# Second block's mixing on one NeuronCore: scans placed among the projections, attention by groups of heads with one row per query, and the output projection in two halves of its inputs

## The reference, cut to what matters

```python
proj = h @ w_in                  # a_q a_k a_v | cq ckv kr | z xbc dt
y_a = diff_attention(a_q, a_k, a_v, lam, subln_g)   # 4 heads, q and k of 32+32, v of 64
y_b = mla(cq, ckv, kr, ...)                         # 4 heads, q and k of 64+32, v of 64
y_c = mamba2(z, xbc, dt, ...)                       # 8 heads of 64
y = concatenate([y_a, y_b, y_c]) @ w_out            # 256 + 256 + 512 inputs
x = x + g * rmsnorm(y)
```

## Time and profile before

| | |
|---|---|
| Median of 3 runs | 3539.12 us (3535.72 to 3542.89) |
| Profiled execution: its own time | 3541.45 us |
| Profiled execution: span | 3539.7 us |
| PE busy | 3192.5 us (90%) |
| DVE busy | 1755.1 us (50%) |
| POOL busy | 832.0 us (24%) |
| ACT busy | 705.4 us (20%) |
| Mean granted PE clock | 0.913 |

### The profile page before, as it was taken

One profiled execution on the slowest core, in us unless ns is written; L12 is line 12 of the kernel. 1 busy time (PEld: TensorE's weight loads), 2 busy tenths in 40 slices (PEclk: granted clock), 3 DMA queues, 4 the chain that ended last, 5 costly groups with the idle time before them and its releaser, 6 DMA issues.

```text
span 3539.7 us, 33580 instructions
## 1 busy us (share of the span) xinstructions
PE 3192.5 (90%) x12312; PEld 2192.8 (62%) x12312; DVE 1755.1 (50%) x3758; ACT 705.4 (20%) x1539; POOL 832.0 (24%) x704
## 2 busy tenths in 40 slices
PE   6877989999987788999979998899997998899996
PEld 3334548888733454888864452488884444378886
DVE  1375337775327543777542265495833347152343
ACT  2233320000113332000012241220202133121110
POOL 0120113444312011344430000144340000124442
PEclk8987799999998788999999978899998978899998
DMA  4111313443211001344221100144420210112221
GB/s 194 57 39 72 143 60 113 173 179 110 90 48 48 24 1 60 130 156 183 106 76 67 71 1 0 72 172 161 179 103 28 76 48 1 48 48 95 77 91 48
DMA packets 38546, 304.89 MB, mean 86 GB/s; under 512 B 4192, under 2 KB 4320, under 8 KB 23920
## 3 DMA queue, kind: packets, MB, share of 16 engines
q1 hardware_dynamic: 38352, 302.68, 23.3%
q0 software_dynamic: 32, 0.07, 0.0%
HBM read 300.63 MB, written 2.10 MB: 86 GB/s over the span
## 4 chain that ended last, share of the span: by engine, by line
PE 78%; DVE 11%; issue 4%; ACT 3%; DMA 2%; POOL 1%; DVEq 0%; SPq 0%; POOLq 0%; ACTq 0%
PE bank L950 43%; PE bank L928 16%; PE bank L1039 4%; PE bank L1294 1%; DVE SPT L2265 1%; PE bank L1147 1%; PE bank L1089 1%; PE bank L1278 1%; PE bank L1076 1%; PE bank L1026 1%; DMA ring<-in_slabs 1%; DVE sel L1931 1%; PE bank L1285 1%; PE bank L1013 1%; DVE m L1930 1%
## 5 line engine op out<-in xcount | busy, mean ns | idle before, releaser
L855 POOL TENSOR_TENSOR SPT<-ring 128x512 f32<-128x512 f32 (+2 forms) x140 | 170.3, 1216 | 1863.3 <-DMA ring<-in_slabs 1244.6
L928 PE MATMUL bank<-hT,ring 128*128 128x512 f32 (+1 forms) x960 | 422.2, 599 | 14.6 <-ACT hT L1604 6.5
L950 PE MATMUL bank<-U,ring 128*128 128x256 f32 x1728 | 406.5, 380 | 0.0
L950 PEld LDWEIGHTS bank<-U,ring 128*128 128x128 f32 x1728 | 326.3, 190 | 43.3
L928 PEld LDWEIGHTS bank<-hT,ring 128*128 128x128 f32 (+1 forms) x960 | 181.3, 190 | 252.1 <-issue 246.1
L1750 DVE SCALAR_TENSOR_TENSOR nw<-sel,c,nw 128x256 f32<-128x256 f32 x504 | 321.8, 638 | 23.2 <-DMA sel<-in_mod_pieces 5.5
L950 PE MATMUL bank<-hT,ring 128*128 128x256 f32 x1216 | 299.8, 397 | 22.4 <-ACT hT L1604 8.6
L950 PE MATMUL bank<-U,SPT 128*128 128x256 f32 x1296 | 311.2, 379 | 0.1
L950 PE MATMUL bank<-hT,SPT 128*128 128x256 f32 x1216 | 287.3, 379 | 0.0
L950 PEld LDWEIGHTS bank<-hT,ring 128*128 128x128 f32 x1216 | 230.3, 195 | 70.9 <-issue 17.2
L950 PEld LDWEIGHTS bank<-U,SPT 128*128 128x128 f32 x1296 | 246.2, 190 | 33.9 <-POOL SPT L860 0.5
(11 more groups left out here) (293 smaller groups left out, 4164.6 us busy)
## 6 DMA issues: line engine op xcount, KB each, us to landing
ring<-in_slabs SPq DMA_DIRECT2D x88, 2048.0 KB, 8.0
sel<-in_mod_pieces SPq DMA_DIRECT2D x144, 512.0 KB, 3.8
ring<-in_slabs SPq DMA_DIRECT2D x8, 1536.0 KB, 7.1
ring<-in_slabs SPq DMA_DIRECT2D x8, 1280.0 KB, 6.0
ring<-in_slabs SPq DMA_DIRECT2D x4, 1664.0 KB, 7.0
ring<-in_slabs SPq DMA_DIRECT2D x2, 1808.0 KB, 7.3
cst<-in_consts SPq DMA_DIRECT2D x1, 2120.0 KB, 24.3
ring<-in_slabs SPq DMA_DIRECT2D x2, 1056.0 KB, 5.3
```

What stands on the lines that cost most here:

```text
L855: pool.tensor_tensor(e1, a21, a22, ALU.add).then_inc(*pool_order.up())
L928: mm = pe.matmul(dst, lhs(k), rhs(k), start=(k == 0), stop=(k == n - 1))
L950: mm = pe.matmul(into[j][:, c:c + HALF], lhs[:, k, :], rhs[:, k, :], start=(begin and k == 0), stop=(end and k == kp - 1))
```

## The change

1. **Order.** `proj` 6 to 9, 4 and 5 come first, then `projv`, then `proj` 0 to 3, 10 to 13 and the mla steps ("dense") are woven with all the scan steps ("scans"). Then `proj` 14 to 17 are woven with `sz`, `sn` and the first six attention slots (the mla groups), and the remaining slots (the 12 diff groups) with the first half of the output projection.
2. **Attention by groups.** 6 mla groups and 12 diff groups of 1 to 4 heads instead of 32 units. No multiplication of the weights by 1/sum: for mla the output is scaled; for diff one combination `cb` per head forms `e1 + c e2`. The value product has one row per query (weights stationary), outputs are normed per query (square on ACT, reduction on DVE, Ln and Exp on ACT, `on` on DVE) and turned back by `ot`.
3. **Output projection** in two halves of its inputs: `("wo", 0, n)` takes the four scan tiles, ACT copies it; `("wo", 1, n)` takes the attention outputs, DVE adds it. Squares are summed by POOL, with one matmul at the end, for `post` 0 as for `post` 1.
4. **Banks.** PROJ (0, 1) for projections; `da` has bank 2 alone, `xd` and `G` bank 3; `y` alternates over 4 and 5; `pv` has bank 6 alone, `ot` and `sn` bank 7. Mixing matrices are packed, three heads deep. Slabs are repacked (`bv` of 4160 columns, `mix` of 1280) and come in another order.

```diff
+GROUPS2 = [("m", 0, 4, 0), ("m", 0, 4, 1), ("m", 0, 2, 2), ("m", 2, 2, 2), ("m", 0, 2, 3), ("m", 2, 2, 3)]
+NM2 = len(GROUPS2)
+GROUPS2 += [("d", h, 2, i) for i in (0, 1) for h in range(2)] + [("d", h, 1, i) for i in (2, 3) for h in range(4)]
...
+    for j in range(len(groups) + 3):
+        slot = []
+        if j < len(groups):
+            slot.append([("sc", groups[j])])
+        if 0 <= j - 1 < len(groups):
+            if GROUPS2[groups[j - 1]][0] == "d":
+                slot.append([("cb", groups[j - 1])])
+            slot.append([("tp", groups[j - 1])])
+        if 0 <= j - 3 < len(groups):
+            slot.append([("on", groups[j - 3])])
+        if 0 <= j - 2 < len(groups):
+            slot.append([("pv", groups[j - 2])])
+        if 0 <= j - 3 < len(groups) and groups[j - 3] in TURNS2:
+            slot.append([("ot", groups[j - 3])])
...
     for n in range(6, 10):
+        o += [st for c in tile2(n) for st in c] + [("conv", n - 6)]
+    for n in (4, 5):
+        o += [st for c in tile2(n) for st in c] + [("conv", n)]
+    o += [("projv", 0), ("projv", 1), ("projv", 2), ("projv", 3), ("dt",), ("silu", 0)]
+    dense = [c for n in range(4) for c in tile2(n)]
+    dense[8] += [("cqss",)]
+    dense += [[("kvss",), ("kr",)]]
+    dense += [c for n in range(10, 14) for c in tile2(n)]
+    dense += [[("silu", 1)]] + [[("mq", h)] for h in range(4)] + [[("mk", h)] for h in range(4)]
+    dense += [[("mqr", h)] for h in range(4)] + [[("mv", i)] for i in range(QT)]
+    scans = [[("dtt",)]] + [[("xd", i)] for i in range(QT)] + [[("G", g, st)] for g in range(2) for st in range(QT)]
+    scans += [[("da", 0)]]
+    for h in range(10):
+        if h < 7:
+            scans.append([("da", h + 1)])
         if h < 8:
+            scans += [[("scan", h, st)] for st in range(QT)]
+        if 0 <= h - 1 < 8:
+            scans.append([("y", h - 1)])
+        if 0 <= h - 2 < 8:
+            scans.append([("yo", h - 2)])
+    o += woven((0.0, 1.0, dense), (0.1, 1.0, scans))
+    slots = group_slots2(range(len(GROUPS2)))
+    keys = [c for n in range(14, 18) for c in tile2(n)]
+    o += woven((0.0, 1.0, keys), (0.0, 0.4, [[("sz",)], [("sn", 0)], [("sn", 1)]]),
+               (0.1, 1.0, [c for slot in slots[:NM2] for c in slot]))
+    o += woven((0.0, 1.0, [[("wo", 0, n)] for n in range(KT)]), (0.0, 1.0, [c for slot in slots[NM2:] for c in slot]))
     for n in range(KT + 1):
         if n < KT:
-            o.append(("wo", n))
+            o.append(("wo", 1, n))
         if n >= 1:
             o.append(("ys", 0, n - 1))
...
+    if kind == "da":
+        return [(st, ROWS[:1])]
+    if kind in ("xd", "G"):
+        return [(st, ROWS[1:])]
+    if kind == "y":
+        return [(st, TURN)]
...
+    if kind == "pv":
+        return [(st, OUT)]
...
# POOL, ahead of the layer's slab_sums; and again behind them
+                add_squares(l, 0)
...
# ACT
+                    elif kind == "on" and GROUPS2[st[1]][0] == "d":
+                        act.wait_ge(*s2["uv"].after(l, g - NM2 + 1))
+                        act.activation(stat[:, 0:nh], stat[:, 28:28 + nh], ACT.Ln).then_inc(*act_order.up())
+                        act.wait_ge(*act_order.last())
+                        act.activation(stat[:, 0:nh], stat[:, 0:nh], ACT.Exp, scale=-0.5).then_inc(*s2["ur"].up())
...
# DVE
+                    elif kind == "wo" and st[1] == 1:
+                        dve.wait_ge(*bk2.ready(l, st))
+                        dve.wait_ge(*bk2.taken(l, ("wo", 0, n)))
+                        dve.tensor_tensor(y, y, src[:, :], ALU.add).then_inc(*freed)
```

More of the change, by code:

```diff
@@ new lines, in head_of, with group_slots2 @@
+def head_of(group, hh):
+    return group[1] + (hh if group[0] == "m" else 2 * hh)
+def group_slots2(groups):
+    out = []
+    for j in range(len(groups) + 3):
[12 more added lines that the diff above has]
+            slot.append([("ot", groups[j - 3])])
+        out.append(slot)
+    return out
@@ L465, in order2, with tile2 @@
+def tile2(n):
+    return [[("proj", 3)]] if n == 3 else [[("pj", n, 0)], [("pj", n, 1)], [("pj", n, 2)], [("proj", n)]]
 def order2(l):
     o = [("prep",), ("ns", 0), ("nh", 0)]
[L467 to L470, removed]
@@ L605, in build @@
         hT = sb("hT", [P, KT, SEQ])
-        ring = sb("ring", [P, RING, SLAB])
+        slots = sb("ring", [P, RING, SLOT])
+        ring = slots[:, :, 0:SLAB]
         U = sb("U", [P, 32, SEQ])
@@ L810, in _ @@
                 w = width(blk, kind, s)
-                sp.dma_start(ring[:, n % RING, 0:w], A["slabs"][n, :, 0:w]).then_inc(landed[n % RING], 16)
+                sp.dma_start(slots[:, n % RING, 0:w], A["slabs"][n, :, 0:w]).then_inc(landed[n % RING], 16)
                 if n == RING - 1:
@@ new lines, in _ @@
+                        if n == 0 and s == 0:
+                            pe.wait_ge(*s2["hn"].after(l, 7))
+                        elif n == 0:
+                            for g in TURNS2:
+                                pe.wait_ge(*bk2.taken(l, ("ot", g)))
+                        pe.wait_ge(*sl2.ready(l, ("wo", s)))
+                        w4 = ring[:, sl2.slot(l, ("wo", s)), :].rearrange("p (k n) -> p k n", k=4)
+                        right = [U[:, XC + t, :] for t in range(4)] if s == 0 else [hT[:, 0, :], hT[:, 1, :], U[:, MO[0], :],
+                                                                                  U[:, MO[1], :]]
@@ L1580, in _ @@
                     kind = st[0]
-                    jobs = jobs2(st)
-                    if jobs:
-                        src = bank[bk2.bank(l, jobs[0][0])]
-                        freed = (free[bk2.bank(l, jobs[0][0])], 1)
+                    home = bk2.bank(l, st) if bk2.has(l, st) else None
+                    src = bank[home] if home is not None else None
+                    freed = (free[home], 1) if home is not None else None
                     if kind == "prep":
```

558 lines of the change are left out of this document (319 added, 239 removed).

## The result

The changed kernel takes 3600.2 us (median of four, 3598.8 to 3604.9) where the kernel before, on the same chip, took 3537.4 (3535.4 to 3542.9): a ratio of 1.0174, 95% interval 1.0157 to 1.0190. The forecast was 3520 with a range up to 3588. The profiled execution took 3604.85 us, its span is 3603.1; the span before was 3539.7, so 63.4 us have to be found.

What follows compares the result with a forecast made beforehand. PE was taken to bound the kernel. Per layer -24.4 + 18.6 - 7 + 3.2 = -9.6 us, -19 for two, from 3539.1 to 3520; own range 3495 to 3532, 8 in 10 within 3462 to 3588.

Steps and rivals of the forecast that it cites:

- the tail: Last output projection product to the feed-forward's first: 3.2 us a layer lost; POOL's queued weight sums at nothing, uncovered 5.
- A: Projections ahead of the weave: six tiles and `projv`, dense on PE, 55.4 us a layer.
- C: `proj` 14 to 17 woven with `sn` and mla groups: 58 us a layer, bounds 50 and 68.
- E: Second half of the output projection: 30.5 us where 37.5 stood, a gain of 7 a layer.
- B: Scans woven with projections: PE bounds at 107 us, with waits 112 a layer, upper bound 125.
- Rival 4: List placed by count, ACT holds tile copies at each `da`: scans woven with projections take 125, total 3546; chance 0.06.
- D: Diff groups woven with the output projection's first half: 117 us a layer at clock about 0.79, bounds 100 and 152.
- The ring: Diff slots: PE, DVE and ACT wait for each other in turn; 6.7 us per 512-key head, fifteen slots 81.
- Rival 1: Dense output projection pieces keep the diff stage at the upper clock, 100 us a layer: total 3486; chance 0.16.
- rival 2: Weaving hides the waits between engines, all parts at PE's work, 304 us a layer: total 3369; chance 0.04.
- Rival 3: Diff stage stays at the lower clock, 152 us, 25 a layer lost: total 3590; chance 0.23 in full or part.
- Loads: Slab loads in another order and the next modulation's weight pieces: no cost; uncovered, a load at most some 8 us.

Runs made afterwards that it cites:

- scans_early: Changed kernel with the scan steps placed over the first nine tenths of the weave with the projections, not the last nine tenths: 3594.0 us.
- on_first: Changed kernel with `on` of group j-3 as the first step of a slot, ahead of the scores, not behind the transposes: 3578.4 us.
- both_d: Changed kernel with `on` first in each slot and the eight output projection pieces right behind the scores of the last eight diff groups: 3508.2 us.
- sums_late: Changed kernel with POOL's first feed-forward weight sums waiting until DVE has updated the last tile of x: 3600.6 us.
- comb2: Changed kernel with `on` first, half pieces behind scores and in draining slots, scans over 0.0 to 0.9, slabs 2 MiB apart, POOL's first sums under the output projection: 3465.4 us.
- b_row: Kernel before the change with only the slabs' DRAM row length raised from 4096 to 4160 numbers: 3548.1 us.
- a_pitch: Changed kernel with slabs 2 MiB apart in DRAM as in the kernel before, the two 4160-column slabs behind all others: 3597.3 us.

## Why the prediction was wrong, step by step

*The measure of the loss.* Forecast were -12.8 us for the mixer per layer, +3.2 for the tail, nothing elsewhere. Measured: +20, +8.1, and 7.5 once.

*A, C and E* came out as forecast: 55.5 to 56.9 for 55.4, 57.5 and 58.1 for 58, 29.4 for 30.5. In C the two waits for `sn`'s squares came as costed (5.6 us for 5.5). The 3 us of value products waiting for `on` did not come, and PE was busy 51.3 us and not 49.6; that these two offset each other is luck.

*B, 112 forecast, 127.6 measured: mis-sized, 15.6.* Three terms. "PE work: 107 us" is 112.6. It counted records at the pitch of long runs, and between products of other kinds two records of 512 columns take 1.05 us for the 0.86 and four take 1.91 for the 1.72; 1 us is a slip, since 133.4 less part A's 55.4 leaves 78 and not 77. "2 us more" for the last steps was 7.3 of waiting and 2.2 for a last `y` that took 4.5 where the others take 2.4. The shared bank's "about 3" was 4.1. These three make 14.2; the other 1.4 is in PE's busy time and was not traced. Rival 4 had the size (125) and half the mechanism: the list is placed by count, but it was DVE that idled, 6.3 us at a rotary part and 2 to 3 at the `da` of three heads, not ACT that held copies. "Scans should be ahead of their use", my argument against it, is what failed. `scans_early` settles the wait. The 26.9 us of the earlier trace rows, read there as PE's idle time, hold the waits of PE's matmuls and those of its weight loads together; PE's own waits for the scans' products are 10.1 us in that layer. The sum does not use the figure, since it prices the old scans by the length of their stage.

*D, 117 forecast, 132.7 measured: the step that failed.* The ring itself stood: 109.5 us without pieces is near my figure for the lower clock, 115. What failed is what I did with the pieces and the clock. I took the clock as an outside number, "at about 0.79", from the first block's stretch, and counted each piece at 3.43, "exposed in full", "hidden", or "half". But the order moved the clock from 0.73 to 0.75, 0.79 and 0.82 in the three reorderings: a piece behind a wait starts at the lower level, and seven of the eight cost 5.2 to 6.0 (42.8 for 27.5 us in all). They add 23.2 us to the bare ring's 109.5, where I added 17.6 and 2 to a ring that I put mostly at the upper level. By my own formula a clock of 0.73 gives 123; no run divides the other 10. The count of the places was off too, the other way: by the list three pieces stand in front of scores, two behind them and three behind `tp` or `pv`, which makes 15.4 us and not 17.6 (and my own count of four, two and two makes 17.2). I had also put `on` behind the transposes down as part of an unavoidable ring; `on_first` shows it was 16 us of order.

*Rival 1 and rival 2* did not come true in the changed kernel. But a D under 100 exists with these very instructions (84.9), once PE has a piece and no wait in a slot. The Trainium skill (TensorE: Matmul & The Clock Gate, Part 1) says that sustained activity releases the throttle. The slot of `both_d`, busy throughout at 1.00, agrees, and so does the changed kernel's 0.73 with 45 us of waits. The old diff stage does not: from 2035 to 2070 PE was busy 34.9 of 35 us, and the clock stayed at 0.50. So the waits do not explain the level in every stretch; what else does stays open.

*Rival 3* (3590 in full) named the right side and stage, and fell 10 us short: D stayed below 152, while B and the tail, which it left alone, lost as well.

*The tail: "I cost them at nothing; uncovered, 5 us."* The size of the uncovered cost was right by luck: not PE waiting for the sums, but DVE slowed beside them, 5.7 us by the passes and 5.3 by the tail of `sums_late`. There the tail is still 2.7 us longer than the old 19.5, which is the root's own way, near the 3.2 forecast. The Trainium skill (GPSIMD Engine Reference, Specifications) says that GpSimd shares its SBUF interfaces with VectorE, with contention for DVE instructions that have two SBUF inputs. The traces agree on both sides: 1.61 to 1.75 for 0.69 to 0.75 with two such inputs, and in `comb2` an unchanged 0.69 for the addition that reads PSUM. I had not looked for it.

*Loads: "nothing".* I had asked only when the ring's slots fall free. The wider slab changed the spacing of all slabs in DRAM, and so the first block: 7.5 us in this execution, 7 and 8 by the times of `b_row` and `a_pitch`, with wide intervals.

## What to carry to other kernels

When work is woven into a ring of engines that wait for each other in turn, place each piece where the engine would wait for the ring's slowest step and nowhere else, and move every step whose inputs are ready a slot early to the slot's front: here the same instructions took 133 and 85 us. Price a filler at the clock of the place where it stands, and the ring at the clock that the fillers leave it. When a chore is moved on POOL, ask which DVE passes it now runs beside, not only who waits for its result.

## What was not expected of the hardware

- Beside POOL passes of 128x512 a DVE pass of that size with two SBUF inputs took 1.63 us for 0.69, and the passes of two other lines were slowed likewise where they met POOL; a DVE pass with one PSUM input stayed at 0.69.
- The gains of two reorderings were more than their sum: 16.2 and 27.0 us alone, 47.8 together, with the clock of the stage at 0.75, 0.79 and 0.82.
- Storing slabs 2,129,920 bytes apart and not 2,097,152 let other transfers (the modulation's pieces) land in 4.8 to 5.2 us for 3.8 to 4.1. The mechanism stays open.
- Halves of 1.7 us in each slot of the diff stage left the clock at its lower level in some slots and not in others, at the same order of work; what decides between them was not found.
